# Experts' outputs added onto the residual rows in memory by the scatter itself, in place of a stage that sums four rows per token

## The reference

```
h2 = rms_norm(x1, norm2_w) * (1 + sc2) + sh2
logits = h2 @ w_router + b_router;  top 4 per token, top_w = softmax of the 4 logits
per token t and chosen expert e:
    gu = h2[t] @ w_gate_up[e] + b_gate_up[e];  gate, up = halves of gu
    act = min(gate, 7) * sigmoid(1.702 * gate) * (clip(up, -7, 7) + 1)
    y[t, e] = act @ w_down[e] + b_down[e]
out[t] = x1[t] + g2 * sum over the 4 experts of top_w[t, e] * y[t, e]
```

## Time and profile before

| | us |
|---|---|
| time, median of 3 runs (lowest to highest) | 2961.32 (2960.67 to 2965.88) |
| the profiled execution, span from its first to its last instruction | 2962.3 |
| PE busy in it | 2595.5 (88%) |
| DVE busy | 1839.1 (62%) |
| ACT busy | 1427.7 (48%) |
| POOL busy | 500.1 (17%) |

### The profile page before, as it was taken

The page is one execution under the profiler, slowest core; times in us unless marked ns, Lnnn a source line. Parts: engine busy times, 40 slices in busy tenths (PEclk is TensorE's granted clock), DMA queues, the critical chain, the costliest instruction groups (busy, mean ns, idle before and its releaser), DMA issues. The chain is left out here.

```text
span 2962.3 us, 39628 instructions
## 1 busy us (share of the span) xinstructions
PE 2595.5 (88%) x11553; PEld 1932.0 (65%) x11554; DVE 1839.1 (62%) x2784; ACT 1427.7 (48%) x2282; POOL 500.1 (17%) x502
## 2 busy tenths in 40 slices
PE   5899959898929999999999999999999999999930
PEld 2688835566827677677766777777667767667720
DVE  1663246664536776755688655755886565876735
ACT  1322114443425656644577544644775464775520
POOL 0121000000131311211122111211231111221100
PEclk9899978997959999999999999999999999999975
DMA  6122043322517877855599555755997575895735
GB/s 202 61 87 77 15 111 98 103 90 70 138 55 237 279 258 246 284 179 191 198 319 324 193 198 190 263 174 187 316 313 241 191 245 191 303 302 191 255 124 231
DMA packets 420768, 572.65 MB, mean 193 GB/s; under 512 B 20722, under 2 KB 319218, under 8 KB 419698
## 3 DMA queue, kind: packets, MB, share of 16 engines
q1 hardware_dynamic: 391906, 496.96, 51.6%
q0 software_dynamic: 20816, 58.33, 5.5%
q10 hardware_dynamic: 8002, 16.80, 1.6%
HBM read 526.93 MB, written 45.12 MB: 193 GB/s over the span
## 5 line engine op out<-in xcount | busy, mean ns | idle before, releaser
L1547 ACT ACTIVATE d_whi<-d_raw 128x1024 fp32r<-128x1024 f32 x528 | 531.1, 1048 | 267.5 <-PE psum L1747 235.2
L1743 PE MATMUL psum<-d_whi,d_xthi 128*128 128x512 f32 x1536 | 632.2, 412 | 19.8 <-DVE d_xtlo L1619 18.8
L1628 DVE TENSOR_TENSOR d_wlo<-d_raw,d_whi 128x1024 fp32r<-128x1024 f32 x462 | 550.9, 1218 | 93.5 <-ACT d_whi L1547 92.1
L1743 PE MATMUL psum<-d_whi,d_xtlo 128*128 128x512 f32 x1536 | 604.7, 394 | 0.0
L1743 PE MATMUL psum<-d_wlo,d_xthi 128*128 128x512 f32 x1536 | 601.3, 391 | 0.0
L1628 DVE TENSOR_TENSOR d_wlo<-slab,d_whi 128x1024 fp32r<-128x1024 f32 x268 | 356.0, 1360 | 131.5 <-ACT d_whi L1547 131.5
L1547 ACT ACTIVATE d_whi<-slab 128x1024 fp32r<-128x1024 f32 x268 | 271.7, 1051 | 210.6 <-PE psum L1747 210.6
L1743 PEld LDWEIGHTS psum<-d_whi,d_xthi 128*128 128x128 f32 x1536 | 288.7, 188 | 122.4 <-issue 63.2
L1743 PE MATMUL psum<-d_whi,d_athi 128*128 128x512 f32 x768 | 314.7, 410 | 22.2 <-DVE d_atlo L1634 22.2
L1743 PEld LDWEIGHTS psum<-d_whi,d_xtlo 128*128 128x128 f32 x1536 | 288.6, 188 | 64.3
L1743 PEld LDWEIGHTS psum<-d_wlo,d_xthi 128*128 128x128 f32 x1536 | 289.5, 188 | 52.6
(11 more groups left out here) (268 smaller groups left out, 3829.2 us busy)
## 6 DMA issues: line engine op xcount, KB each, us to landing
slab<-in_w_gate_up_dram SPq DMA_DIRECT2D x134, 1024.0 KB, 7.8
d_raw<-in_w_gate_up_dram SPq DMA_DIRECT2D x132, 1024.0 KB, 7.8
d_raw<-in_w_down_dram SPq DMA_DIRECT2D x66, 2048.0 KB, 7.7
b_raw<-in_w_ada_dram SPq DMA_DIRECT2D x8, 2048.0 KB, 8.7
e_y<-y_d SPq DMA_DIRECT2D x8, 2048.0 KB, 13.7
slab<-in_w_in_dram SPq DMA_DIRECT2D x12, 1024.0 KB, 5.4
slab<-in_w_ada_dram SPq DMA_DIRECT2D x8, 1024.0 KB, 5.1
a_xin<-in_x_dram ACTq DMA_DIRECT2D x2, 2048.0 KB, 9.1
```

Source lines behind the costliest of these rows:

```text
L1547: nc.scalar.activation(whi[j % 2][:, part, :], raw[j % NRAW][:, part, :], ACT.Copy).then_inc(whi_ok, 1)
L1628: nc.vector.tensor_tensor(wlo[j % 2][:, part, :], raw[j % NRAW][:, part, :], whi[j % 2][:, part, :].bitcast(F32), ALU.subtract).then_inc(w ...
L1743: nc.tensor.matmul(to, m_[b][:, k, :], w_[w][:, k, :], start=(k == 0 and q == 0), stop=False)
```

## The change

The scatter adds its rows onto memory instead of overwriting (compute_op add), and goes to the residual rows themselves: x1 is stored in acc_d, which has 128 padding rows behind it, and y_d is gone. So the rows must be weighted and gated before: the four weights per token are stored to memory by SP at the end of mixer_block (topw_d), POOL gathers the weight of each row of a group (roww, two more indirect DMAs per group), and the output from PSUM is now one DVE instruction (times roww, times gate2) in the place of ACT's copy. List entries have a third number for it. combine_block is replaced by one DMA from acc_d to the output, issued by SP when POOL's last scatter has landed. The padding rows are written once at the start of expert_block.

```diff
@@ shared
-    s.x1_d = dram("x1_d", [s.T, s.D], F32)
+    s.acc_d = dram("acc_d", [s.T + P, s.D], F32)
+    s.topw_d = dram("topw_d", [s.T * s.TOPK + P, 1], F32)
-    s.list_d = dram("list_d", [s.E * s.T, 2], I32)
-    s.y_d = dram("y_d", [s.T * s.TOPK + P, s.D], F32)
+    s.list_d = dram("list_d", [s.E * s.T, 3], I32)
@@ project_block, POOL
-                own.link(nc.gpsimd.memset(nolist[:, :, 0:1], 0))
+                own.link(nc.gpsimd.memset(nolist[:, :, :], 0))
+                for c, base in ((1, T), (2, s.TOPK * T)):
...
@@ mixer_block, SP (end)
+                sp.wait_ge(topw_ok, 1)
+                sp.dma_start(s.topw_d[0:T * K4, :].rearrange("(t p r) a -> p t (r a)", p=P, r=K4),
+                             s.topw_all[:, :, :]).then_inc(topw_st, 16)
+                sp.wait_ge(topw_st, 16)
                 sp.wait_ge(slab_in, 32)
@@ mixer_block, ACT
-                    act.dma_start(s.x1_d[bass.ds(i * P, P), :], xt[b][:, :]).then_inc(x1_st[b], 16)
+                    act.dma_start(s.acc_d[bass.ds(i * P, P), :], xt[b][:, :]).then_inc(x1_st[b], 16)
@@ mixer_block, DVE, place
                         nc.vector.tensor_copy(entry[b][r][:, 0:1], tokf[:, bass.ds(i, 1)])
-                        ins = nc.vector.tensor_scalar(entry[b][r][:, 1:2], tokf[:, bass.ds(i, 1)], float(K4), float(r),
+                        nc.vector.tensor_copy(entry[b][r][:, 1:2], tokf[:, bass.ds(i, 1)])
+                        ins = nc.vector.tensor_scalar(entry[b][r][:, 2:3], tokf[:, bass.ds(i, 1)], float(K4), float(r),
                                                       ALU.mult, ALU.add)
@@ mixer_block, DVE, after the weights
+                dve.sem_inc(topw_ok, 1)
                 dve.wait_ge(cnt_mm, 1)
@@ expert_block, SP (end)
                 load(0, total(sp), 0)
+                sp.wait_ge(added, 1)
+                sp.dma_start(out[0, :, :], s.acc_d[0:T, :]).then_inc(out_st, 16)
+                sp.wait_ge(out_st, 16)
@@ expert_block, POOL (start)
                 own.link(nc.gpsimd.memset(two[:, :], 0))
+                pool.dma_start(s.acc_d[T:T + P, :], yst[0][:, :]).then_inc(pad_st, 16)
+                pool.dma_start(s.topw_d[T * s.TOPK:, :], yst[0][:, 0:1]).then_inc(pad_st, 16)
+                pool.wait_ge(pad_st, 32)
@@ expert_block, POOL, scatter
-                        pool.indirect_dma_start(out=s.y_d[:, :],
+                        pool.indirect_dma_start(out=s.acc_d[:, :],
                                                 out_offset=bass.IndirectOffsetOnAxis(ap=ydst[b][:, :], axis=0),
-                                                in_=yst[b][:, :], in_offset=None).then_inc(y_st[b], 16)
+                                                in_=yst[b][:, :], in_offset=None, compute_op=ALU.add
+                                                ).then_inc(y_st[b], 16)
@@ expert_block, POOL, body
                         own.link(nc.gpsimd.tensor_copy(ydst[b][:, :], entry[b][:, 1:2]))
                         s.settle(pool)
+                        pool.indirect_dma_start(out=roww[b][:, :], out_offset=None, in_=s.topw_d[:, :],
+                                                in_offset=bass.IndirectOffsetOnAxis(ap=entry[b][:, 2:3], axis=0)
+                                                ).then_inc(roww_in[b], 16)
                     own.link(nc.gpsimd.memset(two[:, :], blocks - 1))
                     for b in range(2):
                         pool.wait_ge(xg_in[b], 16 * (g + 1))
+                        pool.wait_ge(roww_in[b], 16 * (g + 1))
                         pool.wait_ge(xt_mm[b], g + 1)
@@ expert_block, ACT: output() and its two calls removed; DVE: the same places in its pass
+                def output(g, jd, b, sh):
+                    dve.wait_ge(dn_mm, CRED + 2 * DN * g + 2 * jd + (b + 1) * sh)
+                    dve.wait_ge(y_st[b], 16 * (g + 1))
+                    dve.wait_ge(roww_in[b], 16 * (g + 1))
+                    cols = slice(jd * SL, (jd + 1) * SL)
+                    nc.vector.scalar_tensor_tensor(yst[b][:, cols], psum[:, 2 * ((GU + jd) % 2) + b, :],
+                                                   roww[b][:, 0:1], s.gate2[:, cols], ALU.mult,
+                                                   ALU.mult).then_inc(y_ok, sh)
...
+                            elif j > GU:
+                                output(g, j - 1 - GU, b, sh)
                         split(g, j + 1, [3] if j < GU else [2, 3])
+                    for b in range(blocks):
+                        output(g, DN - 1, b, sh)
@@ combine_block removed
```

More of the change, by code:

```diff
@@ L247, in _ @@
                 own.link(nc.gpsimd.memset(chanmean[:, :], 1.0 / DC))
-                own.link(nc.gpsimd.memset(nolist[:, :, 0:1], 0))
-                own.link(nc.gpsimd.iota(nolist[:, :, 1:2].rearrange("p (a n) c -> p a (n c)", n=P),
-                                        pattern=[[0, s.E * T // P // P], [1, P]], base=s.TOPK * T, channel_multiplier=0))
+                own.link(nc.gpsimd.memset(nolist[:, :, :], 0))
+                for c, base in ((1, T), (2, s.TOPK * T)):
+                    own.link(nc.gpsimd.iota(nolist[:, :, c:c + 1].rearrange("p (a n) c -> p a (n c)", n=P),
+                                            pattern=[[0, s.E * T // P // P], [1, P]], base=base,
+                                            channel_multiplier=0))
                 own.link(nc.gpsimd.memset(s.ones_row[:, :], 1.0))
@@ L901, in mixer_block @@
         iota_e = sb("c_iota_e", [P, E], F32)
-        entry = [[sb(f"c_entry{i}_{r}", [P, 2], I32) for r in range(K4)] for i in range(2)]
+        entry = [[sb(f"c_entry{i}_{r}", [P, 3], I32) for r in range(K4)] for i in range(2)]
         tokf = sb("c_tokf", [P, NT], F32)
@@ L1288, in _, with expert_block @@
                                  stop=True).then_inc(cnt_mm, 1)
-def expert_block(nc, s, a):
+def expert_block(nc, s, a, out):
     T, D, KT, E = s.T, s.D, s.KT, s.E
@@ L1321, in expert_block @@
         xg = [sb(f"d_xg{b}", [P, D], F32) for b in range(2)]
-        entry = [sb(f"d_entry{b}", [P, 2], I32) for b in range(2)]
+        entry = [sb(f"d_entry{b}", [P, 3], I32) for b in range(2)]
+        roww = [sb(f"d_roww{b}", [P, 1], F32) for b in range(2)]
+        roww_in, pad_st, added, out_st = ([sem(f"d_roww_in{b}") for b in range(2)], sem("d_pad_st"),
+                                          sem("d_added"), sem("d_out_st"))
         ydst = [sb(f"d_ydst{b}", [P, 1], I32) for b in range(2)]
@@ L1464, in _ @@
                 for b in range(2):
-                    own.link(nc.gpsimd.iota(ydst[b][:, :], pattern=[[0, 1]], base=s.TOPK * T, channel_multiplier=1))
+                    own.link(nc.gpsimd.iota(ydst[b][:, :], pattern=[[0, 1]], base=T, channel_multiplier=1))
                 own.link(nc.gpsimd.memset(yst[0][:, :], 0.0))
                 own.link(nc.gpsimd.memset(two[:, :], 0))
+                pool.dma_start(s.acc_d[T:T + P, :], yst[0][:, :]).then_inc(pad_st, 16)
+                pool.dma_start(s.topw_d[T * s.TOPK:, :], yst[0][:, 0:1]).then_inc(pad_st, 16)
+                pool.wait_ge(pad_st, 32)
                 start = own.n
@@ L1530, in _ @@
                 s.settle(pool)
+                pool.sem_inc(added, 1)
             @block.scalar
@@ L1562, in sigmoid @@
                     nc.scalar.activation(sg[b][:, :], gate[b][:, :], ACT.Sigmoid, scale=ALPHA).then_inc(sg_ok, sh)
-                def output(g, jd, b, sh):
-                    act.wait_ge(dn_mm, CRED + 2 * DN * g + 2 * jd + (b + 1) * sh)
-                    act.wait_ge(y_st[b], 16 * (g + 1))
-                    nc.scalar.activation(yst[b][:, jd * SL:(jd + 1) * SL], psum[:, 2 * ((GU + jd) % 2) + b, :],
-                                         ACT.Copy).then_inc(y_ok, sh)
                 def turned(g, j, b, sh):
@@ L1598, in body @@
                                 turned(g, j - 1, b, sh)
-                            elif j > GU:
-                                output(g, j - 1 - GU, b, sh)
                         split(g, j + 1, [3] if j < GU else [2, 3])
-                    for b in range(blocks):
-                        output(g, DN - 1, b, sh)
                 xt(0, 1)
@@ L1851, in build @@
             s.release(nc)
-        expert_block(nc, s, arrays)
-        s.release(nc)
-        combine_block(nc, s, arrays, out)
+        expert_block(nc, s, arrays, out)
 _INS = ['x', 'c', 'w_ada', 'b_ada', 'norm1_w', 'w_in', 'b_forget', 'q_norm_w', 'k_norm_w', 'conv_w',
```

59 lines of the change are left out of this document (2 added, 57 removed).

## The result

| | us |
|---|---|
| before, median (lowest to highest) of 4 runs | 2960.99 (2959.93 to 2965.88) |
| after, median (lowest to highest) of 4 runs | 2981.72 (2980.74 to 2983.27) |
| ratio after / before, with its 95% interval | 1.0068 (1.0054 to 1.0082) |
| profiled execution after, span | 2979.7 |

The forecast was 2951 us. The change costs 0.7% where 0.3% less was expected.

The account below looks back on a forecast made before the run. The prediction took PE to bound the expert stage, with POOL on the path in one-block groups. Terms -87 + 4 + 50 + 37 - 14 = -10 took 2962.3 to 2952, and 2951 us as median; range 2890 to 3012.

Parts of the forecast that it names:

- one-block groups: PE's wait for slab 2's pieces: 5.0 us more in each of 10 groups (50 us), 4.6 in 8 others (37 us).
- Last stage: End of the kernel: 117 us become 30, of which the final copy takes 21; a gain of 87 us.
- Start: Start of the expert stage: POOL issues two padding stores and waits for their landing; a loss of 4 us.
- POOL's chain after the scatter: Scatter to slab 2's pieces: start at 17.3 us, not 9.95, after one block; 17.4, not 10.5, after two.
- The output's later start, taken as hidden: Output on DVE after one-block groups: the scatter leaves 1.9 us later, assumed covered by the 2 MB load's landing.
- rival 3: One-block groups: the scatter's later start counts, 19 us more, giving 2970 us; chance 0.11.
- Two-block groups: Output moved from ACT to DVE: ACT turns block 1's rows sooner, sparing PE stalls; a gain of 14 us.
- the first (2871): Rival on one-block groups: POOL's chain stays nearly covered, late by 1.0 us in 10 groups; 2871 us, chance 0.25.
- the second, the dear add (3004): Rival on the scatter's landing in 18 groups: the adding scatter costs 5.3 us over again; 3004 us, chance 0.22.

Follow-up runs that it names:

- e8_reorder_pad: e4_reorder with POOL's wait for the two padding-row stores moved from the start of the expert stage to just before the first scatter; 2848.66 us.
- e1_plain: The changed kernel with the scatter storing instead of adding, the sum left out of the result; 2954.62 us.
- b2_gathers: The kernel before, with two unused 1 KB gathers put between POOL's copies of row numbers and waited for ahead of slab 2's pieces; 3044.97 us.
- b3_dve_out: The kernel before, with only the output moved from ACT to DVE, its factors a constant and gate2; 2963.13 us.
- e3_act_out: The changed kernel with the output back on ACT, the multiplication by gate2 left out; 2988.47 us.
- e2_warm: The changed kernel with 28 useless extra matmuls keeping PE busy in its one-block-group stall before slab 2's third piece; 2965.96 us.
- e4_reorder: The changed kernel with POOL's pieces of slab 2 put ahead of its waits for the scatter's landing and the weights and the row-number copies; 2842.32 us.
- b1_reorder: The kernel before, with POOL's wait for the scatter's landing and the row-number copies moved behind the pieces of slab 2; 2964.62 us.
- e6_reorder_out: e4_reorder with DVE's first output of a group put ahead of xt_low instead of behind it; 2844.26 us.

## Why the prediction was wrong

Its main mechanism is there: POOL's chain in one-block groups decides. The steps in its order:

- **Last stage**, -87 forecast, -93 measured. The landing was sized well (7.5 us from the second scatter's issue to the copy's, 9.0 forecast); the copy took 15.6 us and not 21. The prediction counted its bytes twice, read and written, against a rate of a view that counts them once: in the window of the copy (the second row at the top) 300 GB/s x 14 us are the 4.19 MB, at a share of 0.88. The window of the last stage before, 223 GB/s x 113 us = 25.2 MB, is also its loads and stores counted once. Counted once, the copy comes to 13 us at 331 GB/s, which the prediction has as its lower bound. (The scatter at 2845.32, from which the prediction counts, is the last one and not the second last.)
- **Start**, +4 forecast, +0.3 measured. This came out by luck. POOL waited 10.5 us for the padding stores, where 3.2 us were forecast, but the stage began 5.4 us earlier (861.27 us in place of 866.65): POOL stands 5.0 us at the border of the two stages and not 10.6. It is 5.0 to 5.5 in all the runs built on the changed kernel and 10.6 to 11.5 in those built on the kernel before; the cause is open. e8_reorder_pad takes 4.9 us out of the wait.
- **POOL's chain after the scatter**, sized right after one block: the landing ended at 9.7 (9.6 forecast) and the pieces started at 16.9 (17.3). Inside it two errors cancel: the second gather was issued at 13.8 (13.1), with 0.8 us in front of each gather and not 0.3, and the pieces started 3.1 us after that (4.2). The gathers held POOL for 1.16 us in the median, not 1.34. After two blocks the chain was 1 us too short: the pieces start at 18.4 on average (17.4 forecast). Of the period, e1_plain gives 1.3 us to the add and b2_gathers 5.3 at the most to the gathers.
- **The output's later start, taken as hidden: this step failed.** The prediction had it hidden because the landing ends with the 2 MB load in front of it. b3_dve_out shows the whole 2.05 us arriving at the pieces, 1.3 us of it in the period after one block. e3_act_out shows some cover: of the 1.7 us that it took off, 1.1 were given back by pieces that start later after the scatter. It is rival 3, which had been priced at 19 us; the two experiments, measured at PE, put it at 9 to 15.
- **What PE does behind the stall: a term that was missing.** The prediction charged PE with the time of standing still and with nothing for the clock, which falls to 0.50. 12 matmuls at 0.43 in place of 0.23 us are 2.4 us a group; e2_warm gives the net, 1.1 us in each of 18 groups, 19 us.

For the 10 one-block groups after one block the account, in means, closes so: POOL's pieces start 6.97 us later after the scatter, the scatter 2.06 later after PE, and the first of them is 0.71 faster (2.33 in place of 3.04). The third piece of the slab is thus there 8.3 us later. Before, PE came to it 1.0 us after it was ready, and now it takes it up at once, so PE is 7.36 late there. Behind it another 0.68 are lost: the clock's 2.4, of which half lies beside POOL's last piece, less some 0.5 of PE's waits that went. That is 8.04 measured at PE. The forecast was 5.0, with 0.4 for the faster pieces and 1.9 for the waits. That is 30 of the 49 us by which one-block groups exceed the forecast (136 measured at PE, 87 forecast). After two blocks the excess is 2.4 us a group: 1.2 of it is the chain, 8.1 us longer and not 6.9, and 1.1 the clock, by e2_warm.

- **Two-block groups**, -14 forecast, -26 measured at PE. b3_dve_out, the move alone, gives -16, near the forecast. The other 10 are 0.7 us in each of 14 groups, and they are in b2_gathers too, where the output is on ACT (78.22 in place of 78.88, 76.82 in place of 77.51). They come from matmuls that start closer together: in two-block groups behind another such group 226.6 ns apart on average and not 229.5, in some 263 steps a group. That is so in the changed kernel, e3_act_out, e4_reorder and b2_gathers, and not in b1_reorder or b3_dve_out. The former have the weight gathers, or b2's stand-ins, with their small tiles on the chip, the latter have neither; whether the gathers or the moved tiles do it stays open.

Of the rivals the first (2871) is refuted by the pieces' start, and the second, the dear add (3004), by e1_plain: the add costs 30 us in all, less than the 10 x 1.9 + 8 x 3.2 + 3.2 = 48 that the forecast itself had put in for it. The errors sum to the miss: +49 on one-block groups, -12 on two-block groups, -6 on the last stage, -4 on the start, which is 27 us, and 2979.7 - 2952 is 28.

e4_reorder settles the cause: the same work in an order that puts nothing between ACT's half and POOL's pieces removes 142 us. Its profiled span of 2838.1 is 124 us below the kernel before: -93 at the end, -25 in two-block groups and -7 in one-block groups, measured at PE. That profiled execution is one of the fastest of this kernel (2839.77 us, median 2842.32).

## What to carry to other kernels

An engine that is busy for a fifth of the time (POOL here, 592 of 2980 us) can set the pace, if its program has a wait for a far transfer ahead of work that others need. Before adding to such a chain, count from the last event upstream to the due time downstream, take each delay of the start at its full length as long as nothing shows it covered, and add the clock that a standing TensorE loses. Better, move the due work ahead of the wait: here that order alone, which gained nothing in the kernel before (b1_reorder), turned a loss of 0.7% into a gain of 4%.

## What the runs showed of the hardware

- An adding scatter of 128 rows of 4 KB holds POOL for 1.63 us in the median and 1.00 without the add. In 11 of the 18 scatters behind a one-block group it is some 2.6 us, and 2.0 without the add (e1_plain); in e3_act_out, where DVE does not write the outputs, and in e6_reorder_out, where it writes the first one earlier, the same scatters take 1.6 to 1.7. Which of DVE's instructions beside them does it, no run separates. The 0.5 KB load issued right behind an adding scatter takes 1.19 us in the median in place of 0.56; behind a plain one it took 0.57 in e1_plain and 0.56 in b3_dve_out, even behind scatters of 2.0 us.
- A gather of 128 rows of 4 bytes landed after 2.4, 3.6 and 6.0 us (least, median, most) in the changed kernel. Issued right behind the scatter, in e4_reorder, it landed after 3.8, 6.4 and 9.5, and held POOL for 1.96 us in the median in place of 1.16.
- One DMA of 4.19 MB from memory to memory took 15.6 us from its issue to the end of the span: 269 GB/s with each byte counted once, as the views do, and 538 GB/s read and written together.
- With POOL's chain out of the way a one-block group has DMA busy for 0.99 of its 42.84 us, and 0.95 of 43.10 in the kernel before, at 318 and 316 GB/s. That DMA bounds the group is not shown: PE and ACT wait for no slab there.
